# The last product of a hybrid encoder block as seven block products of sums, with its weights in quarters of 512 columns

## The chip, the cores and the metric

The kernel runs on one core of a Trainium2 chip. The metric is the time of one execution on the device in microseconds (us); lower is better. Several executions of the kernel before were timed, and one execution of it was profiled; its trace is what is read below. Engines: TensorE (PE in the profile; its weight loads are PEld), VectorE (DVE), ScalarE (ACT), GpSimd (POOL), SyncE (SP), which here only issues transfers.

## The reference

One layer: RMSNorm, one wide projection, sparse attention, a state-space layer, then two projections merged by sigmoid gates, the product with `w_out`, the residual and a final RMSNorm. Sequence 512, model width 2048, float32. What the change touches is the end:

```python
gates = jax.nn.sigmoid(merge + b_merge).reshape(bsz, l, N_BRANCH, D_MODEL)
mixed = gates[:, :, 0] * y_a + gates[:, :, 1] * y_b      # 512 x 2048
return x + mixed @ w_out                                 # w_out: 2048 x 2048
...
return rms_norm(x, g_final)
```

## The kernel before

Everything is kept transposed, channels on the 128 partitions and the 512 tokens along the free dimension, in 16 rows `k` of 128 channels. Each float32 operand is split in two parts, a rounded high part and the low rest, and each product is three matmuls (high by high, high by low, low by high), each with a 128x128 stationary and a 128x512 moving operand. The high part is made by ScalarE (a copy that rounds, `high_through`, L703), the low part by VectorE (a subtraction in place of the raw weights, `low_through`, L992). Weights stream in units of 128x2048 through three slots (`w_raw`, `w_hi`, `w_lo`; `w_raw` and `w_lo` are the same memory). SyncE issues the load of a unit when TensorE is done with the unit three before (`load`, L308). All orders are written out by hand: each engine has its list of instructions, and semaphores hold them together.

Before the last product comes `merge1`: 16 tiles of 128 channels (j = 0 to 15), each 48 matmuls. After each tile ScalarE makes the sigmoid gate (L709), VectorE multiplies and adds (L1380, L1381) and so finishes one row of `mixed` in `ya`. Rows of `ya` are then split by ScalarE (L923) and VectorE (`low_of_merge`, L1374).

The last product (`out_bank`, L655 to L657) runs in two halves of 1024 output columns. In a half all eight PSUM banks are in use: four tiles of 128 tokens by two of 512 columns. TensorE goes through k = 0 to 15, and for each k through all eight banks: 3 x 8 x 16 = 384 matmuls a half, 768 in all. The stationary operand is `mixed`, the moving one the weights. The last k rows of a half are done bank by bank, so that banks come free one after the other. VectorE adds each bank to the residual `res` (L1392), ScalarE takes the sums of squares (L951, L957, L961), and at the end of the second half VectorE and ScalarE scale the tokens (L1419 to L1424, L965) and SyncE stores them. `res` is loaded from `x` (L360) into the memory of `yb` once the merge is done, and the final gain `g_last` behind it (L363). GpSimd does nothing in this part.

## Time and profile before

| | us |
|---|---|
| time, median of 3 runs | 1188.05 (1187.62 to 1188.37) |
| the profiled execution, its own time | 1186.81 |
| span of its trace (first to last instruction) | 1185.0 |
| TensorE busy | 1158.0 (98%) |
| VectorE busy | 752.5 (64%) |
| ScalarE busy | 403.4 (34%) |
| GpSimd busy | 11.8 (1%) |

The span is 1.8 us shorter than the execution's own time. A matmul's record is longer than its place in the stream (they are pipelined), so TensorE's pace is read from the starts of consecutive matmuls. The same holds for back-to-back instructions of VectorE and ScalarE: a merged row with x12 gives the time of all twelve together. "Idle before" names who ended an engine's wait.

### The profile page before, as it was taken

The numbers are of one execution on the slowest core, as the hardware profiler recorded it, in microseconds if no ns is written. First come the engines' busy times: TensorE is split into PE (matmuls) and PEld (weight loads), VectorE is DVE, ScalarE is ACT, GpSimd is POOL, SyncE is SP. The second block draws the span as 40 slices with busy tenths as digits, with TensorE's granted clock in tenths as the row PEclk, the third lists the DMA queues.
The fourth block names the chain that finished last, engine by engine and source line by source line (L and its number), as shares of the span: only waits on it lengthen the run. The fifth ranks groups of instructions, "written<-read, shape, count | busy, mean of one in ns | idle before, by whom it ended". The sixth has DMA issues, their size and how long they took to land.

```text
span 1185.0 us, 13271 instructions
## 1 busy us (share of the span) xinstructions
PE 1158.0 (98%) x5357; PEld 949.8 (80%) x5357; DVE 752.5 (64%) x1317; ACT 403.4 (34%) x526; POOL 11.8 (1%) x12
## 2 busy tenths in 40 slices
PE   5999999999999999999999999999999999999997
PEld 4999888888777788887777777788888888887886
DVE  5887568999777778628999999443133343423324
ACT  7423243332376543332222323233222223313114
POOL 3000000000000000000000000000000000000000
PEclk9999999999999999999999999999999999999999
DMA  7444323223332237443433443332443343245223
GB/s 248 107 107 108 106 72 101 77 76 103 98 115 90 72 98 216 131 137 110 139 107 107 137 130 90 106 103 76 107 107 87 92 107 104 77 169 219 78 101 142
DMA packets 171885, 134.86 MB, mean 114 GB/s; under 512 B 10968, under 2 KB 158768, under 8 KB 170672
## 3 DMA queue, kind: packets, MB, share of 16 engines
q1 hardware_dynamic: 162912, 124.73, 36.1%
q10 hardware_dynamic: 8912, 9.29, 2.2%
q8 instruction: 42, 0.69, 0.2%
q14 instruction: 19, 0.16, 0.0%
HBM read 121.42 MB, written 12.58 MB: 113 GB/s over the span
## 4 chain that ended last, share of the span: by engine, by line
PE 83%; DVE 13%; DMA 1%; ACT 1%; issue 1%; SPq 0%; DVEq 0%; ACTq 0%
PE bank L405 21%; PE bank L407 20%; PE bank L406 20%; PE bank L655 5%; PE bank L657 5%; PE bank L656 5%; DVE w_lo L992 3%; DVE score L1097 2%; DVE small L1096 2%; PE bank L557 1%; PE bank L597 1%; PE bank L538 1%; DVE score L1085 1%; DMA xt<-in_x 1%; PE bank L547 1%
## 5 line engine op out<-in xcount | busy, mean ns | idle before, releaser
L405 PE MATMUL bank<-act_hi,w_hi 128*128 128x512 f32 (+1 forms) x1088 | 422.5, 388 | 2.6 <-DVE w_lo L992 2.6
L406 PE MATMUL bank<-act_lo,w_hi 128*128 128x512 f32 (+1 forms) x1088 | 416.9, 383 | 0.0
L407 PE MATMUL bank<-act_hi,w_lo 128*128 128x512 f32 (+1 forms) x1088 | 416.9, 383 | 0.0
L992 DVE TENSOR_TENSOR w_lo<-w_raw,w_hi 128x2048 fp32r<-128x2048 f32 x96 | 219.6, 2288 | 177.9 <-ACT w_hi L703 177.0
L703 ACT ACTIVATE w_hi<-w_raw 128x2048 fp32r<-128x2048 f32 (+1 forms) x97 | 184.8, 1905 | 184.1 <-DMA w_raw<-in_w_out 104.9
L405 PEld LDWEIGHTS bank<-act_hi,w_hi 128*128 128x128 f32 x1088 | 204.4, 188 | 48.5 <-issue 9.6
L407 PEld LDWEIGHTS bank<-act_hi,w_lo 128*128 128x128 f32 x1088 | 204.3, 188 | 38.5
L406 PEld LDWEIGHTS bank<-act_lo,w_hi 128*128 128x128 f32 x1088 | 204.5, 188 | 34.7
L655 PE MATMUL bank<-w_hi,act_hi 128*128 128x512 f32 x192 | 74.7, 389 | 0.0
L656 PE MATMUL bank<-w_lo,act_hi 128*128 128x512 f32 x192 | 74.7, 389 | 0.0
L657 PE MATMUL bank<-w_hi,act_lo 128*128 128x512 f32 x192 | 74.7, 389 | 0.0
L1380 DVE TENSOR_TENSOR gate<-gate,yb 128x512 f32<-128x512 f32 x16 | 11.1, 692 | 97.3 <-ACT gate L709 97.3
L709 ACT ACTIVATE gate<-bank,g_cols 128x512 f32<-128x512 f32 x16 | 11.0, 688 | 134.1 <-PE bank L407 134.1
L773 ACT ACTIVATE relu<-bank 128x256 f32<-128x256 f32 (+2 forms) x48 | 23.6, 492 | 90.9 <-PE bank L506 84.7
L405 PE MATMUL bank<-a_hi,w_hi 128*128 128x512 f32 x128 | 50.0, 390 | 0.0
L407 PE MATMUL bank<-a_hi,w_lo 128*128 128x512 f32 x128 | 49.8, 389 | 0.0
L406 PE MATMUL bank<-a_lo,w_hi 128*128 128x512 f32 x128 | 49.8, 389 | 0.0
L1085 DVE SCALAR_TENSOR_TENSOR score<-relu,w_idx,score 128x256 f32<-128x256 f32 (+2 forms) x45 | 27.8, 618 | 29.0 <-ACT relu L773 27.8
L656 PEld LDWEIGHTS bank<-w_lo,act_hi 128*128 128x128 f32 x192 | 36.0, 188 | 7.5
L655 PEld LDWEIGHTS bank<-w_hi,act_hi 128*128 128x128 f32 x192 | 36.0, 188 | 7.5
L657 PEld LDWEIGHTS bank<-w_hi,act_lo 128*128 128x128 f32 x192 | 36.0, 188 | 7.4
L405 PE MATMUL bank<-s_hi,w_hi 128*128 128x512 f32 x80 | 31.1, 389 | 0.0
(249 smaller groups left out, 1300.9 us busy)
## 6 DMA issues: line engine op xcount, KB each, us to landing
w_raw<-in_w_in SPq DMA_DIRECT2D x68, 1024.0 KB, 5.6
w_raw<-in_w_out SPq DMA_DIRECT2D x16, 1024.0 KB, 5.5
e_tables<-e_made ACTq DMA_DIRECT2D x16, 512.0 KB, 2.9
w_raw<-in_w_att_out SPq DMA_DIRECT2D x8, 1024.0 KB, 5.9
e_tab<-e_tables SPq DMA_DIRECT2D x16, 512.0 KB, 6.5
xt<-in_x SPq DMA_DIRECT2D x4, 1024.0 KB, 8.1
w_raw<-in_w_ssm_out SPq DMA_DIRECT2D x4, 1024.0 KB, 5.0
res<-in_x SPq DMA_DIRECT2D x4, 1024.0 KB, 11.7
```

The source lines that it names most:

```text
L405: nc.tensor.matmul(out_ap, wh, x_hi[k], start=(j == 0), stop=False)
L406: nc.tensor.matmul(out_ap, wh, x_lo[k], start=False, stop=False)
L407: last = nc.tensor.matmul(out_ap, wl, x_hi[k], start=False, stop=(j == n - 1))
L655: nc.tensor.matmul(out_ap, mh, w_hi[:, slot, w], start=(k == 0), stop=False)
L656: nc.tensor.matmul(out_ap, mh, w_lo[:, slot, w], start=False, stop=False)
L657: last = nc.tensor.matmul(out_ap, ml, w_hi[:, slot, w], start=False, stop=(k == KD - 1))
L703: nc.scalar.activation(w_hi[:, u % SLOTS, 0:n_el], w_raw[:, u % SLOTS, 0:n_el], ACT.Copy).then_inc(high_done, 1)
L773: nc.scalar.activation(relu[:, n % 2, 0:(b + 1) * P], pair_bank[n % 2][:, 0:(b + 1) * P], ACT.Relu, scale=IDX_DIM ** -0.5).then_inc(relu_d ...
L992: v.tensor_tensor(w_lo[:, u % SLOTS, :], w_raw[:, u % SLOTS, :], w_hi[:, u % SLOTS, :].bitcast(F32), ALU.subtract).then_inc(split_done, 1)
L1085: ins = v.scalar_tensor_tensor(scores[b], r, w, scores[b], ALU.mult, ALU.add)
L1096: link(v.max(small[:, 12:20], scores[b]))
L1097: link(v.match_replace(scores[b], small[:, 12:20], scores[b], REPLACED))
```

## The change

Rows (tokens) and columns of `mixed` and of the weights are cut in two, and per half of 1024 output columns the 2x2 block product is done with seven block products in place of eight, in Winograd's form of Strassen's scheme (15 sums). The two blocks in k are k = 0 to 7 and 8 to 15; those in tokens 0 to 255 and 256 to 511; those in columns two times 512.

- Four sums of `mixed` are made for each k of 0 to 7 (`sums_of`), in the memory of `yb`; the merge takes its rows in the order `MERGE_ORDER`, so that k and k + 8 are done together. Each operand is split as before.
- Weights are loaded in quarters of 128x512, in a ring of 12 (the same three slots). A half is 16 blocks of work: n = 0 to 7 with three quarters each (B11, B12, B22, from which two sums are made), n = 8 to 15 with four each (three sums); `turned` makes the sums on VectorE in place, then ScalarE and VectorE split each quarter. The second half is n = 16 to 31.
- The first eight blocks of a half fill six banks (products 1 to 3), the second eight use two more for product 4 and then reuse the six. Before that, `kept1`, `u2` and `u4` are taken out of them (ScalarE once, VectorE `mix`), and GpSimd adds them to `res`.
- The rows of `mixed` that are not split by the end of the merge are split between blocks 2 to 5 (`SPLIT_AT`).
- `res` is loaded in two halves, behind the quarters of block 7 (when all splits are done) and behind those of block 10. `g_last` is loaded behind the quarters of block 29.
- The last two blocks are done for 128-token tiles 0 and 2 first, then for 1 and 3; the tokens are finished in the order 2, 0, 3, 1.

The diff, cut to its core, indented less by twelve blanks:

```diff
-("ssmout", 4, 4), ("merge1", 14, 1), ("out", 16, 1)]
+("ssmout", 4, 4), ("merge1", 14, 1), ("out", 0, 1)]
 EARLY = 2
+HALF_K = KD // 2
+MERGE_ORDER = [0, 1, HALF_K, HALF_K + 1] + [k + HALF_K * i for k in range(2, HALF_K) for i in range(2)]
+RING = 4 * SLOTS
+HALVES = SEQ // 2
...
+def block_at(n):
+    half, second, k = n // (2 * HALF_K), n // HALF_K % 2, n % HALF_K
...
-        LAST_UNIT = UNIT0["out"] + 16
+        LAST_UNIT = UNIT0["out"]
+        BLOCKS = 4 * HALF_K
+        LAST_ORDER = (3, 0, 1, 2)
+        SPLIT_ORDER = [(0, k) for k in range(5)] + [(0, 5), (1, 0), (1, 1), (0, 6), (1, 2), (1, 3), (0, 7), (1, 4), (1, 5), (1, 6), (1, 7)]
+        SPLIT_AT = {2: SPLIT_ORDER[5:8], 3: SPLIT_ORDER[8:11], 4: SPLIT_ORDER[11:14], 5: SPLIT_ORDER[14:16]}
+        LAST_TOKENS = (2, 0, 3, 1)
+        a_banks, b_banks, c_banks, d_banks = banks[0:2], banks[2:4], banks[4:6], banks[6:8]
...
+def load_quarter(g, k, col):
+    if g < RING:
+        sp.wait_ge(tile_done, tiles_through(LAST_UNIT - SLOTS + g // 4))
+    else:
+        sp.wait_ge(q_done, 2 * (g - RING + 1))
+    slot, part = ring(g)
+    sp.dma_start(w_raw[:, slot, part], w_out_v[:, k, col:col + 512]).then_inc(q_loaded[g % RING], 16)
...
+for n in range(BLOCKS):
+    half, second, k = block_at(n)
+    b11, b12, b21, b22 = ((k + HALF_K * i, half * HALF + 512 * j) for i in range(2) for j in range(2))
+    for i, (kk, col) in enumerate((b11, b21, b22, b12) if second else (b11, b12, b22)):
+        load_quarter(quarter_at(n) + i, kk, col)
+    if n == 7:
+        sp.wait_ge(m_low, 2 * HALF_K)
+        load_res(0, range(TOK))
+    if n == 10:
+        load_res(1, range(TOK))
+    if n == BLOCKS - 3:
+        sp.wait_ge(shared_added, 16)
+        sp.dma_start(g_last[:, :], g_final.rearrange("(a d) -> a d", a=1).to_broadcast([P, D])).then_inc(gf_loaded, 16)
...
+for half in range(2):
+    pool.wait_ge(res_loaded[half], 16 * TOK)
+    if half:
+        pool.wait_ge(bank_taken, 8)
+    col = half * HALF
+    for ready, sources, into in ((p1_saved, kept1, ((0, 0),)), (u2_made, u2, ((2, 0),)), (u4_made, u4, ((0, 512), (2, 512)))):
+        for tb in range(2):
+            pool.wait_ge(ready, 2 * half + tb + 1)
+            for t, c in into:
+                part = res[:, t + tb, col + c:col + c + 512]
+                pool.tensor_tensor(part, part, sources[:, tb, :], ALU.add).then_inc(shared_added, 1)
...
+def first_pass(n, i, tb):
+    half, _, k = block_at(n)
...
+    if half == 1 and k == 0:
+        pe.wait_ge(bank_taken, (4, 6, 8)[i])
+    return block_product(bank[tb], quarter_at(n) + i, m_hi, m_lo, k == 0, k == HALF_K - 1)
+def second_pass(n, i, tb):
+    half, _, k = block_at(n)
...
+    if k == 0:
+        if i == 0 and half == 1:
+            pe.wait_ge(bank_taken, 2)
+        if i >= 1:
+            pe.wait_ge((p1_saved, u4_made, u2_made)[i - 1], 2 * half + 2)
+    return block_product(bank[tb], quarter_at(n) + i, m_hi, m_lo, k == 0, k == HALF_K - 1)
+for n in range(BLOCKS - 2):
+    half, second, k = block_at(n)
+    if n == 0:
+        pe.wait_ge(tile_free, TILE0["out"])
     if half == 0:
+        pe.wait_ge(m_low, SPLIT_ORDER.index((second, k)) + 1)
+    for i in range(4 if second else 3):
+        pe.wait_ge(q_split, quarter_at(n) + i + 1)
+        for tb in range(2):
+            (second_pass if second else first_pass)(n, i, tb).then_inc(q_done, 1)
+for tb in range(2):
+    for n in (BLOCKS - 2, BLOCKS - 1):
+        pe.wait_ge(q_split, quarter_at(n) + 4)
+        for i in LAST_ORDER:
+            second_pass(n, i, tb).then_inc(q_done, 1)
...
+def high_of_first(k):
+    act.wait_ge(sums_made, 2 * k + 2)
+    nc.scalar.activation(ya_r[:, k, HALVES:SEQ], ya[:, k, 0:HALVES], ACT.Copy)
+    nc.scalar.activation(sums12(k)[0], yb[:, k, :], ACT.Copy).then_inc(m_high, 1)
+def high_of_second(k):
+    row = HALF_K + k
+    nc.scalar.activation(act_hi[:, row, :], ya[:, row, :], ACT.Copy)
+    nc.scalar.activation(act_lo[:, k, :], yb[:, row, :], ACT.Copy).then_inc(m_high, 1)
+def high_of_quarters(n):
+    second = block_at(n)[1]
+    for i in range(4 if second else 3):
+        g = quarter_at(n) + i
+        slot, part = ring(g)
+        made = ((3, 0, 0, 1) if second else (0, 1, 2))[i]
+        if made:
+            act.wait_ge(t_made, turned_at(n) + made)
+        else:
+            act.wait_ge(q_loaded[g % RING], 16 * (g // RING + 1))
+        nc.scalar.activation(w_hi[:, slot, part], w_raw[:, slot, part], ACT.Copy).then_inc(q_high, 1)
...
+for n in range(2, BLOCKS):
+    half, second, k = block_at(n)
+    high_of_quarters(n)
+    for which, kk in SPLIT_AT.get(n, ()):
+        (high_of_first, high_of_second)[which](kk)
+    if second and k == 1:
+        if half:
+            act.wait_ge(shared_added, 8)
+        for tb in range(2):
+            act.wait_ge(q_done, done_at(n - 2, 0, tb))
+            nc.scalar.activation(kept1[:, tb, :], a_banks[tb][:, :], ACT.Copy).then_inc(p1_saved, 1)
...
+def sums_of(k):
...
+    v.tensor_tensor(s3, a11, a21, ALU.subtract)
+    link(v.tensor_tensor(s1, a21, a22, ALU.add))
+    v.tensor_tensor(s2, s1, a11, ALU.subtract).then_inc(sums_made, 1)
+    dve.wait_ge(sums_made, 2 * k + 1)
+    v.tensor_tensor(s4, a12, s2, ALU.subtract).then_inc(sums_made, 1)
+def low_of_first(k):
+    hi, lo = sums12(k)
+    dve.wait_ge(m_high, SPLIT_ORDER.index((0, k)) + 1)
+    v.tensor_tensor(ya_r[:, k, 0:HALVES], ya[:, k, 0:HALVES], ya_r[:, k, HALVES:SEQ].bitcast(F32), ALU.subtract)
+    v.tensor_tensor(lo, yb[:, k, :], hi.bitcast(F32), ALU.subtract).then_inc(m_low, 1)
+def low_of_second(k):
+    row = HALF_K + k
+    dve.wait_ge(sums_made, 2 * k + 2)
+    dve.wait_ge(m_high, SPLIT_ORDER.index((1, k)) + 1)
+    v.tensor_tensor(ya_r[:, row, :], ya[:, row, :], act_hi[:, row, :].bitcast(F32), ALU.subtract)
+    v.tensor_tensor(act_lo[:, row, :], yb[:, row, :], act_lo[:, k, :].bitcast(F32), ALU.subtract).then_inc(m_low, 1)
+def turned(n):
+    second = block_at(n)[1]
+    g, t0 = quarter_at(n), turned_at(n)
+    w = [w_raw[:, ring(g + i)[0], ring(g + i)[1]] for i in range(4 if second else 3)]
+    def loaded(i):
+        dve.wait_ge(q_loaded[(g + i) % RING], 16 * ((g + i) // RING + 1))
+    if second:
+        b11, b21, b22, b12 = w
+        loaded(2)
+        loaded(3)
+        v.tensor_tensor(b12, b22, b12, ALU.subtract).then_inc(t_made, 1)
+        loaded(0)
+        dve.wait_ge(t_made, t0 + 1)
+        v.tensor_tensor(b11, b11, b12, ALU.add).then_inc(t_made, 1)
+        loaded(1)
+        dve.wait_ge(t_made, t0 + 2)
+        v.tensor_tensor(b11, b21, b11, ALU.subtract).then_inc(t_made, 1)
+    else:
+        b11, b12, b22 = w
+        loaded(0)
+        loaded(1)
+        v.tensor_tensor(b12, b12, b11, ALU.subtract).then_inc(t_made, 1)
+        loaded(2)
+        dve.wait_ge(t_made, t0 + 1)
+        v.tensor_tensor(b22, b22, b12, ALU.subtract).then_inc(t_made, 1)
+def low_of_quarters(n):
+    for i in range(4 if block_at(n)[1] else 3):
+        g = quarter_at(n) + i
+        slot, part = ring(g)
+        dve.wait_ge(q_high, g + 1)
+        v.tensor_tensor(w_lo[:, slot, part], w_raw[:, slot, part], w_hi[:, slot, part].bitcast(F32), ALU.subtract
+                        ).then_inc(q_split, 1)
...
+    if j == KD - 1:
+        for n in range(2):
+            turned(n)
+            low_of_quarters(n)
...
+    if j == EARLY or j % 2 == 1 and j > EARLY:
+        dve.wait_ge(gate_used, KD + j + 1)
+        sums_of(j // 2 - (j == EARLY))
...
+low_of_first(4)
+turned(2)
...
+def mix(half):
+    n = 2 * HALF_K * half + HALF_K - 1
+    if half:
+        dve.wait_ge(shared_added, 8)
+    for tb in range(2):
+        dve.wait_ge(q_done, done_at(n, 2, tb))
+        dve.wait_ge(p1_saved, 2 * half + tb + 1)
+        v.tensor_tensor(u2[:, tb, :], b_banks[tb][:, :], kept1[:, tb, :], ALU.add).then_inc(u2_made, 1)
+    for tb in range(2):
+        dve.wait_ge(u2_made, 2 * half + tb + 1)
+        v.tensor_tensor(u4[:, tb, :], c_banks[tb][:, :], u2[:, tb, :], ALU.add).then_inc(u4_made, 1)
...
+for n in range(2, BLOCKS):
+    half, second, k = block_at(n)
+    low_of_quarters(n)
+    for which, kk in SPLIT_AT.get(n, ()):
+        (low_of_first, low_of_second)[which](kk)
+    if second and k == 1:
+        mix(half)
+    if n == 2 * HALF_K + 1:
+        take_first_half()
+    if n >= BLOCKS - 2:
+        dve.wait_ge(gf_loaded, 16)
+        dve.wait_ge(first_squared, 2 * TOK)
+        for t in (2 * (n - BLOCKS + 2), 2 * (n - BLOCKS + 2) + 1):
+            v.tensor_tensor(res[:, t, 0:HALF], res[:, t, 0:HALF], g_last[:, 0:HALF], ALU.mult).then_inc(first_scaled, 1)
+    if n + 1 < BLOCKS:
+        turned(n + 1)
...
+def late_tokens(tb):
+    t, i = 2 + tb, 2 * tb
+    if tb:
+        dve.wait_ge(final_rest_done, i - 1)
+    bank = last_bank(tb, 3)
+    add_part(t, HALF + 512, bank).then_inc(part_ready, 1)
+    link(add_part(t, HALF, bank))
+    dve.wait_ge(part_ready, 2 * i + 1)
+    multiplied(i, t, HALF + 512)
+    add_part(t, HALF, last_bank(tb, 0)).then_inc(part_ready, 1)
+    dve.wait_ge(part_ready, 2 * i + 2)
+    multiplied(i, t, HALF)
+def early_tokens(tb):
+    t, i = tb, 2 * tb + 1
+    if tb:
+        dve.wait_ge(final_rest_done, i - 1)
+    for c, b in ((0, 1), (1, 2)):
+        add_part(t, HALF + 512 * c, last_bank(tb, b)).then_inc(part_ready, 1)
+        dve.wait_ge(part_ready, 2 * i + c + 1)
+        multiplied(i, t, HALF + 512 * c)
...
+dve.wait_ge(shared_added, 16)
+late_tokens(0)
+early_tokens(0)
+finish(0)
+late_tokens(1)
+finish(1)
+early_tokens(1)
+finish(2)
+finish(3)
```

How the instructions stand. On VectorE behind the last gate (L1380 and L1381 before, L1570 and L1571 after). Before (L992 splits a unit of weights, L1374 a row of `mixed`, L1392 takes a bank):

```order
L1380 TENSOR_TENSOR gate<-gate,yb 128x512 [waits tile_free]
L1381 TENSOR_TENSOR ya<-ya,gate 128x512 [waits v_step]
L992 TENSOR_TENSOR w_lo<-w_raw,w_hi 128x2048 [waits high_done]
L1374 TENSOR_TENSOR act_lo<-ya,act_hi 128x512 [waits m_high] x12
L992 TENSOR_TENSOR w_lo<-w_raw,w_hi 128x2048 [waits high_done] x6
L1396 MEMSET small 128x1 x4
```

After, the blocks 3 and 4 in the same place (L1545 and L1548 make sums of weights, L1556 splits quarters, L1510 to L1519 split `mixed` and its sums):

```order
L1545 TENSOR_TENSOR w_raw<-w_raw 128x512 [waits q_loaded10,q_loaded9]
L1548 TENSOR_TENSOR w_raw<-w_raw 128x512 [waits t_made,q_loaded11]
L1556 TENSOR_TENSOR w_lo<-w_raw,w_hi 128x512 [waits q_high] x3
L1510 TENSOR_TENSOR ya_r<-ya,ya_r 128x256 [waits m_high]
L1511 TENSOR_TENSOR act_hi<-yb,act_hi 128x512
L1518 TENSOR_TENSOR ya_r<-ya,act_hi 128x512 [waits m_high,sums_made]
L1519 TENSOR_TENSOR act_lo<-yb,act_lo 128x512
L1518 TENSOR_TENSOR ya_r<-ya,act_hi 128x512 [waits m_high,sums_made]
L1519 TENSOR_TENSOR act_lo<-yb,act_lo 128x512
L1545 TENSOR_TENSOR w_raw<-w_raw 128x512 [waits q_loaded1,q_loaded0]
L1548 TENSOR_TENSOR w_raw<-w_raw 128x512 [waits t_made,q_loaded2]
L1556 TENSOR_TENSOR w_lo<-w_raw,w_hi 128x512 [waits q_high] x3
```

The twelve splits of `mixed` in one run became splits of two and two rows between the weights of consecutive blocks, and each block's weights have sums ahead of their splits.

On TensorE at a point where banks change hands. Before, the start of the second half (`bank_taken` counts VectorE's additions):

```order
L655 MATMUL bank2<-w_hi_53,s_hi_112 128x512 [waits bank_taken,split_done]
L655 MATMUL bank3<-w_hi_53,s_hi_112 128x512 [waits bank_taken]
L655 MATMUL bank4<-w_hi_53,s_hi_112 128x512 [waits bank_taken]
L655 MATMUL bank5<-w_hi_53,s_hi_112 128x512 [waits bank_taken]
L655 MATMUL bank6<-w_hi_53,s_hi_112 128x512 [waits bank_taken]
```

After, the first matmuls of block 8 on six of its eight banks (block 24 reads alike), each the first of three:

```order
L724 MATMUL bank6<-w_hi_53,act_hi_49 128x512 [waits q_split,m_low]
...
L724 MATMUL bank0<-w_hi_53,act_hi_49 128x512 [waits p1_saved,q_split]
...
L724 MATMUL bank1<-w_hi_53,act_hi_49 128x512 [waits p1_saved]
...
L724 MATMUL bank4<-w_hi_53,act_lo_50 128x512 [waits u4_made,q_split]
...
L724 MATMUL bank5<-w_hi_53,act_lo_50 128x512 [waits u4_made]
...
L724 MATMUL bank2<-w_hi_53,act_lo_50 128x512 [waits u2_made,q_split]
```

TensorE now waits in the middle of a half too, for a copy of ScalarE (`p1_saved`) and four additions of VectorE (`u2_made`, `u4_made`).

On SyncE, whose transfers go out in this order. Before, from the weights of the last product on:

```order
L308 DMA w_raw<-in_w_out 128x2x1024 [waits tile_done] x8
L360 DMA res<-in_x 128x2048 [waits gate_used]
L360 DMA res<-in_x 128x2048 x3
L363 DMA g_last<-in_g_final 128x2048 [waits m_low]
L308 DMA w_raw<-in_w_out 128x2x1024 [waits tile_done] x8
```

After:

```order
L410 DMA w_raw<-in_w_out 128x512 [waits tile_done] x12
L410 DMA w_raw<-in_w_out 128x512 [waits q_done] x12
L414 DMA res<-in_x 128x1024 [waits m_low]
L414 DMA res<-in_x 128x1024 x3
L410 DMA w_raw<-in_w_out 128x512 [waits q_done] x12
L414 DMA res<-in_x 128x1024 x4
L410 DMA w_raw<-in_w_out 128x512 [waits q_done] x68
L429 DMA g_last<-in_g_final 128x2048 [waits shared_added]
L410 DMA w_raw<-in_w_out 128x512 [waits q_done] x8
```

16 loads of weights became 112 of a quarter of the size (28 units' worth in place of 16), and the residual's first half stands ahead of the weights of block 8.

## Rows read from the trace of the kernel before

**Rows 1.** The page: its first line and busy time of two engines (us, share, instructions)

```profile
span 1185.0 us, 13271 instructions
PE 1158.0 (98%) x5357; PEld 949.8 (80%) x5357; DVE 752.5 (64%) x1317; ACT 403.4 (34%) x526; POOL 11.8 (1%) x12
```

**Rows 2.** The page: the chain that ended last, by engine

```profile
PE 83%; DVE 13%; DMA 1%; ACT 1%; issue 1%; SPq 0%; DVEq 0%; ACTq 0%
```

**Rows 3.** Windows: stretch, length, busy PE, PEld, DVE, ACT, POOL, clock, DMA share, GB/s

```profile
1000.00:1050.00 50.00, 50.00 (x223) 41.40 (x222) 19.98 (x19) 16.30 (x18) 0.00 (x0) 1.00 0.33 100
...
1100.00:1150.00 50.00, 50.00 (x222) 41.43 (x221) 11.57 (x6) 7.67 (x4) 0.00 (x0) 1.00 0.35 105
```

**Rows 4.** Timeline, PE, ACT and DVE at the last merge tile (start, length, what, idle)

```profile
1002.13 0.39 PE L407 MATMUL bank<-act_hi,w_lo 128*128 128x512 f32 x1
...
1002.36 0.39 PE L655 MATMUL bank<-w_hi,s_hi 128*128 128x512 f32 x1
...
1002.62 0.69 ACT L709 ACTIVATE gate<-bank,g_cols 128x512 f32<-128x512 f32 x1 [8.38 <-PE bank L407]
...
1003.34 0.69 DVE L1380 TENSOR_TENSOR gate<-gate,yb 128x512 f32<-128x512 f32 x1 [6.78 <-ACT gate L709]
...
1004.06 0.69 DVE L1381 TENSOR_TENSOR ya<-ya,gate 128x512 f32<-128x512 f32 x1
```

**Rows 5.** Timeline of the tail: TensorE's last matmul, VectorE and ScalarE behind it

```profile
1177.27 0.39 PE L657 MATMUL bank<-w_hi,act_lo 128*128 128x512 f32 x1
1177.76 0.69 DVE L1392 TENSOR_TENSOR res<-bank,res 128x512 f32<-128x512 f32 x1 [1.22 <-PE bank L657]
...
1179.90 1.15 ACT L965 ACTIVATE res<-fin,small 128x1024 f32<-128x1024 f32 x1 [0.30 <-DVE small L1421]
```

**Rows 6.** Timelines of DVE and ACT: twelve instructions back to back

```profile
1007.35 7.30 DVE L1374 TENSOR_TENSOR act_lo<-ya,act_hi 128x512 fp32r<-128x512 f32 x12
...
1005.01 6.35 ACT L923 ACTIVATE act_hi<-ya 128x512 fp32r<-128x512 f32 x12
```

**Rows 7.** Groups by form from 960 us on (busy us, mean ns, idle before)

```profile
L992 DVE TENSOR_TENSOR w_lo<-w_raw,w_hi 128x2048 fp32r<-128x2048 f32 x19 | 43.5, 2290 | 97.6 <-ACT w_hi L703 97.6
...
L1392 DVE TENSOR_TENSOR res<-bank,res 128x512 f32<-128x512 f32 x16 | 10.4, 683 | 7.4 <-PE bank L657 7.3
...
L1409 DVE TENSOR_TENSOR res<-res,g_last 128x1024 f32<-128x1024 f32 x4 | 4.6, 1219 | 2.4 <-ACT square_out L951 2.4
```

**Rows 8.** Groups by form, VectorE, the whole span: 256 columns

```profile
L1141 DVE TENSOR_TENSOR e_temp<-e_base,rot 128x256 f32<-128x256 f32 x4 | 1.7, 424 | 0.1
```

**Rows 9.** Timeline, PE between the two halves

```profile
1089.17 0.39 PE L657 MATMUL bank<-w_hi,act_lo 128*128 128x512 f32 x1
1090.35 0.47 PE L655 MATMUL bank<-w_hi,s_hi 128*128 128x512 f32 x1 [0.80 <-DVE res L1392]
```

**Rows 10.** The page: issues, KB each and us from issue to landing

```profile
w_raw<-in_w_out SPq DMA_DIRECT2D x16, 1024.0 KB, 5.5
```

**Rows 11.** Timelines of SP and ACT around the loads of the residual

```profile
1057.36 2.42 SPq L360 DMA_DIRECT2D res<-in_x  x4
...
1067.83 0.38 SPq L308 DMA_DIRECT2D w_raw<-in_w_out  x1
...
1078.89 1.92 ACT L703 ACTIVATE w_hi<-w_raw 128x2048 fp32r<-128x2048 f32 x1 [14.12 <-DMA w_raw<-in_w_out]
```

**Rows 12.** Windows while the residual is loaded (columns as in Rows 3)

```profile
1064.00:1066.00 2.00, 2.00 (x10) 1.68 (x9) 1.20 (x1) 0.77 (x1) 0.00 (x0) 1.00 0.97 410
```

**Rows 13.** Windows behind TensorE's last matmul (columns as in Rows 3)

```profile
1179.00:1180.00 1.00, 0.00 (x0) 0.00 (x0) 0.45 (x3) 0.67 (x4) 0.00 (x0) 0.93 0.00 0
1180.00:1181.00 1.00, 0.00 (x0) 0.00 (x0) 0.65 (x1) 1.00 (x1) 0.00 (x0) 0.50 0.00 0
```

**Rows 14.** Timeline, POOL: its longest instruction

```profile
23.55 4.60 POOL L395 TENSOR_TENSOR w_lo<-w_raw,w_hi 128x2048 fp32r<-128x2048 f32 x1
```

240 lines of the change are left out of this document (116 added, 124 removed).

## The prediction

> **What bounds the kernel now.** I read the page first. TensorE is busy for 98% of the span [rows 1], and the chain that ended last runs over it for 83% and over VectorE for 13% [rows 2]. Then the windows of the stage that changes: from 1000 us on TensorE has no gap, VectorE works 20 of 50 us, later 11.6, and ScalarE 16 and 8 [rows 3]. So the stage is TensorE's, and fewer matmuls would shorten it, as long as the others keep up. The timelines give its length. The last product starts at 1002.36, one slot behind the last merge matmul [rows 4]; the last matmul of its first half starts at 1089.17 [rows 9]: 384 matmuls in 87.04 us, 0.2267 us each. The second half starts at 1090.35, after a gap of 0.95 us behind VectorE's additions, and its last matmul at 1177.27 ends its slot at 1177.50 [rows 5, 9]. From there to the end of the span are 7.5 us. The stage takes 182.64 us from 1002.36 to 1185.0; I count from 1002.36 as zero.
>
> **What it saves.** Seven products for eight: 32 blocks, half with three and half with four products, six matmuls each, are 672 matmuls for 768. 96 x 0.2267 = 21.8 us. A block of the first kind (n = 0 to 7, 16 to 23) takes TensorE 18 x 0.2267 = 4.08 us, of the second kind 5.44.
>
> **What VectorE must do for a block.** Its additions of 128x512 take 0.69 alone, 0.60 back to back (twelve in 7.30 [rows 6]) and 0.72 start to start where the second waits for the first (1003.34 to 1004.06 [rows 4]). First kind: one sum that the next waits for, one more, three low parts: 0.72 + 0.60 + 3 x 0.60 = 3.12. Second kind: three sums in a chain end after 2 x 0.72 + 0.69 = 2.13; only then ScalarE may round the quarter that it has first in its order (0.62 by the twelve in 6.35 [rows 6], 0.03 for each hand-over [rows 4]), so the first low part starts at 2.81, and four make 5.21. Before, a unit cost 2.29 per 10.9 us of TensorE [rows 7]. VectorE is now at 3.12 of 4.08 and 5.21 of 5.44: anything more comes out of its lead. Added up with no wait at all, VectorE's list is: 2.4 (the last gate), 1.6 (the last four sums), 0.9 (a split), 14 x 3.12 = 43.7, 16 x 5.21 = 83.4, splits 12.4 (below), two mixes 4.8, ten additions from banks 6.0, four multiplications 4.6 (1.14 back to back, 1.22 alone [rows 7]), then 22.6 for the last tokens (below): 182.4, which is the 182.6 of before. So the change can hardly gain even if VectorE never waits.
>
> **Start, +1.1.** Product 1 goes into the banks that the merge's gates are read from, so TensorE waits for the last gate, which ends at 1003.31 [rows 4], and starts at 1.07. Before it began with other banks. Blocks 0 and 1 are turned and split ahead of the last gate, where VectorE has 6.8 us idle [rows 4].
>
> **Blocks 3 to 6, +6.4.** Behind the last gate VectorE has the four sums (256 columns, 0.42 each [rows 8], 1.6 with their waits) and a split (0.34 + 0.60), and begins block 2 at 4.9. A split of the first kind is 0.94, of the second 1.20; blocks 2, 3 and 4 carry 3.34 of these each, block 5 2.40. So VectorE begins block 3 at 11.4, 4 at 17.9, 5 at 24.3, 6 at 29.8, 7 at 33.0, 8 at 36.1; the first quarter is ready 2.0 later and TensorE starts 0.1 behind that. TensorE wants blocks 3, 4, 5, 6 at 13.3, 17.6, 24.1 and 30.5 and gets them at 13.5, 20.0, 26.5 and 32.0: waits of 0.2, 2.4, 2.4 and 1.4. It ends block 7 at 40.1. Before, the twelve splits ran in one piece under matmuls that had their weights.
>
> **Block 8, the load, +3.7.** SyncE waits for the last split (29.9), issues four loads of `res` (0.6 each [rows 11]), then the quarters of block 8. What a queue does behind such loads is in the trace: weights issued at 1067.83 behind them arrived at 1078.9, 11 us, while alone a unit lands in 5.5 [rows 10, 11]; bytes moved at 410 GB/s [rows 12]. 2.1 MB and 1.05 MB at that rate are 7.7 us, from about 31.9 (1.9 after the issue; 5.5 less 2.6 for the bytes leaves 2.9, of which I put 1.9 ahead and 0.7 behind) to 40.2. Without the load VectorE would start at 36.1. The first quarter is ready at 43.7, TensorE waits 3.7. If the queue let the weights pass, this would be 0.
>
> **Block 8, the banks, +6.6.** Products 2 and on in block 8 wait for ScalarE's `kept1`, which stands behind all of block 9 in its list, and for four additions of VectorE, also behind block 9. VectorE starts block 9 at 45.4, ScalarE ends its last quarter at 49.8 and the two copies at 51.0; TensorE had stopped at 45.2: 5.9. VectorE ends the additions at 53.1: 0.7 more. Then it is ahead, and 7 blocks run at 5.44.
>
> **Clock, +1.0.** After the last matmul the granted clock was 0.93 in the slice from 1179 and 0.50 after [rows 13]: it fell from 2.4 to 1.2 GHz some 2.2 us after the last matmul ended. So it falls in the 5.9 too, and the six matmuls behind take about twice as long, partly under the 0.7. I take 1.0, bounds 0 and 3. The waits of 2.4 may do it as well, but VectorE is the later one there.
>
> **Half to half, -0.25.** VectorE takes ten additions between the halves, and most can go while TensorE still works on the later products; I find 0.7 of waiting, for the last two banks, against 0.95 before.
>
> **Block 24, +2.7.** The same two waits as in block 8, with VectorE ahead this time: the ring frees block 25's last quarters when block 22 is half done, their loads take 3, so VectorE starts 25 some 2.4 before block 24 begins, and TensorE waits 2.0 for the copies and 0.7 for the additions.
>
> **Last blocks, +2.4.** Block 31 of the first token tile wants all its quarters 2.7 behind the start of block 30. VectorE has two multiplications by the gain (2.3) ahead of it and gets them ready at 5.1.
>
> **The last tokens, +9.0.** VectorE is free of block 31 and its multiplications 7.2 after the start of block 30. Then it does 18 linked instructions for the four tokens, and twice waits for ScalarE to free `fin`: the third token starts at 15.1, the fourth at 20.3, the last scaling on ScalarE (1.15 [rows 5]) ends at 25.8, and from there to the end it was 3.95 before (1181.05 to 1185.0): 29.8, with TensorE's end at 13.3. That is 16.5 behind the last matmul, 7.5 before.
>
> **Sum.** -21.8 + 1.1 + 6.4 + 3.7 + 6.6 + 1.0 - 0.25 + 2.7 + 2.4 + 9.0 = +10.9. The profiled execution took 1186.81, 1.2 below the median; so 1197.7 for it, and 1199 for the median. Everything before 1002 is as it was: the extra sums and splits in the merge (1.6 + 0.94 for every two tiles) fit in VectorE's idle time (6.78 a tile [rows 4]).
>
> **Rivals.**
> *GpSimd slows VectorE.* GpSimd adds 16 times 128x512 to `res`; by its 4.60 for 2048 columns [rows 14] that is 1.15 each. No row here shows it beside a two-input instruction of VectorE from memory, so its cost to VectorE is between 0 and all of it. Six of eight in a half fall on such instructions: 6.9 us. VectorE's lead behind block 9 is about 4.9, so some 2 are lost in each half, and as VectorE then has no slack left, block 30 comes 3.6 late: +7.6, that is 1206.5. The Trainium skill (SBUF — State Buffer, "two separate sides") says the two share a port pair under an exclusive lock when VectorE reads two inputs from this memory and GpSimd reads it too, and whoever comes second waits for the whole instruction. By that rule this rival is what happens; against it, GpSimd may be the one that waits.
> *The waits are milder.* The load of `res` doesn't hold up block 8, the clock doesn't fall, ScalarE's copies overlap better: what is left is VectorE's list, +0 to +6, some 1192.
> *TensorE stays the bound.* If VectorE's small instructions overlap more than 0.60 each, so that a block with splits costs it under 4.08 and block 31 is ready on time, all stalls go but the start and the tail: -21.8 + 1.1 + 9.0 = -11.7, 1176.3, faster. It decides at 4.08 us per block with splits (6.46 by the rows), which the rows speak against.
> *It doesn't do what it says.* TensorE's list is 96 rows shorter, so this is out.
>
> **How the numbers follow.** The forecast (1195 to 1203) 0.45; GpSimd 0.27; milder 0.17; TensorE-bound 0.05; something dearer than all this (over 1210) 0.06. The range 1190 to 1209 leaves the last two and the ends of others out. A difference under 0.2% (2.4 us) can't be told from none. Faster 0.05; same, from the low end of the milder case, 0.05; slower 0.90.
>
> **What would show it.** In the profile after: 96 matmuls fewer at the same 0.227; TensorE idle behind `w_lo` in blocks 4 to 6 by 1 to 3 us each, behind a load in block 8, then some 6 behind `kept`; VectorE at 90% and more in the stage; a clock below 1 near the wait for `kept`; a tail of about 16 us. GpSimd's additions longer than 1.2 us, or VectorE's of 0.69 stretched to 1.8, would be the first rival. Wrong it would be if TensorE had no gaps in the first half.

## The result, and the profile after

| | before | after |
|---|---|---|
| time, median (lowest to highest) of 4 | 1187.84 us (1187.46 to 1188.37) | 1214.11 us (1213.93 to 1215.02) |
| ratio, 95% interval | | 1.0222 (1.0205 to 1.0240), slower |
| span of the trace | 1185.0 us | 1212.4 us |

The change costs 26.3 us. The forecast was 11 us, with a range up to 1209; the direction was right, the size was not.

The page of the changed kernel: span, busy time, and the chain that ended last.

```profile
span 1212.4 us, 13655 instructions
...
PE 1148.7 (95%) x5261; PEld 937.4 (77%) x5261; DVE 875.6 (72%) x1553; ACT 444.5 (37%) x642; POOL 37.7 (3%) x28
...
PE 70%; DVE 23%; ACT 3%; issue 2%; DMA 2%; SPq 0%; ACTq 0%; DVEq 0%
```

TensorE has 96 matmuls fewer, 5261 for 5357 [rows 1]. But VectorE's part of the chain is 23% instead of 13% [rows 2]: the engine that worked in TensorE's shadow now sets part of the time. The windows over the changed stage (columns as in Rows 3) show it:

```profile
1000.00:1050.00 50.00, 37.71 (x161) 29.37 (x159) 39.39 (x68) 24.82 (x47) 0.00 (x0) 0.99 0.58 186
1050.00:1100.00 50.00, 45.71 (x183) 36.93 (x184) 43.55 (x61) 19.27 (x36) 12.96 (x8) 0.87 0.61 195
1100.00:1150.00 50.00, 43.95 (x179) 35.02 (x178) 43.26 (x67) 17.35 (x30) 6.50 (x5) 0.93 0.51 157
```

Where [rows 3] had TensorE busy for all of 50 us with 222 or 223 matmuls, there are 160 to 183 now, VectorE works 39 to 44 us of 50 instead of 12 to 20, and the granted clock is 0.87 in the middle. Where TensorE stood is read from its timeline. All its waits of 1.3 us and more in the stage are these; in brackets the idle time and who ended it. The last row is its last matmul.

```profile
1023.71 0.47 PE L724 MATMUL bank<-w_hi,ya_r 128*128 128x512 f32 x1 [2.19 <-DVE w_lo L1556]
1030.27 0.47 PE L724 MATMUL bank<-w_hi,ya_r 128*128 128x512 f32 x1 [2.18 <-DVE w_lo L1556]
1035.97 0.47 PE L724 MATMUL bank<-w_hi,ya_r 128*128 128x512 f32 x1 [1.36 <-DVE w_lo L1556]
1049.93 0.77 PE L724 MATMUL bank<-w_hi,act_hi 128*128 128x512 f32 x1 [5.56 <-DVE w_lo L1556]
1050.50 0.63 PE L725 MATMUL bank<-w_lo,act_hi 128*128 128x512 f32 x1
1050.92 0.63 PE L726 MATMUL bank<-w_hi,ya_r 128*128 128x512 f32 x1
...
1057.12 0.76 PE L724 MATMUL bank<-w_hi,act_hi 128*128 128x512 f32 x1 [4.29 <-DVE w_lo L1556]
...
1106.04 0.47 PE L724 MATMUL bank<-w_hi,ya_r 128*128 128x512 f32 x1 [3.77 <-DVE res L1584]
...
1143.96 0.47 PE L724 MATMUL bank<-w_hi,act_hi 128*128 128x512 f32 x1 [2.06 <-DVE w_lo L1556]
...
1186.29 0.79 PE L724 MATMUL bank<-w_hi,act_lo 128*128 128x512 f32 x1 [4.62 <-DVE w_lo L1556]
...
1195.71 0.39 PE L726 MATMUL bank<-w_hi,act_lo 128*128 128x512 f32 x1
```

Every wait names VectorE. (At 1057.12 the name stands for the ScalarE copies: the matmul waited for `p1_saved`, and `kept1` ended at 1056.97.) Behind five of the longer waits the matmuls start some 0.43 us apart (1050.50 to 1050.92), not 0.227. Now the ledger (what each term of the sum took), counted from the end of the last merge matmul's slot as in the prediction; that end is 1003.42, where it was 1002.36. This 1.06 us is a difference between executions and not a cost of the change: in the traces of the versions below, which are the same up to there, the end lies anywhere from 1002.30 to 1004.15. A gap is counted above the pace of 0.2267:

| term | forecast | measured |
|---|---|---|
| 96 matmuls fewer | -21.8 | -21.8 |
| start | +1.1 | +1.0 |
| blocks 3 to 6 | +6.4 | +6.5 |
| block 8, load | +3.7 | +5.7 |
| block 8, banks | +6.6 | +4.7 |
| half to half | -0.25 | +3.0 |
| block 24 | +2.7 | +2.8 |
| blocks 30 and 31 | +2.4 | +6.2 |
| matmuls at half rate | +1.0 | +9.3 |
| tail | +9.0 | +9.0 |
| sum | +10.9 | +26.4 |

The stage takes 208.98 us instead of 182.64. Five terms came out within 0.1. Those that failed are the load, the banks, the boundary between the halves, the last blocks, and the clock. TensorE's list says where it stood, though, not why. The term that grew most, the matmuls at half rate, is tested below in block 8, and there it cost nothing.

The second reading is VectorE's own. Its timeline and GpSimd's behind block 9:

```profile
1053.09 0.69 DVE L1540 TENSOR_TENSOR w_raw<-w_raw 128x512 f32<-128x512 f32 x1
1054.48 2.50 DVE L1556 TENSOR_TENSOR w_lo<-w_raw,w_hi 128x512 fp32r<-128x512 f32 x4 [0.69 <-ACT w_hi L1028]
...
1060.07 1.59 DVE L1537 TENSOR_TENSOR w_raw<-w_raw 128x512 f32<-128x512 f32 x1
1061.76 1.58 DVE L1540 TENSOR_TENSOR w_raw<-w_raw 128x512 f32<-128x512 f32 x1
1064.04 6.10 DVE L1556 TENSOR_TENSOR w_lo<-w_raw,w_hi 128x512 fp32r<-128x512 f32 x4 [0.70 <-ACT w_hi L1028]
1070.06 0.68 DVE L1534 TENSOR_TENSOR w_raw<-w_raw 128x512 f32<-128x512 f32 x1
```

```profile
1059.31 10.29 POOL L473 TENSOR_TENSOR res<-res,u 128x512 f32<-128x512 f32 x6
```

While GpSimd adds shared parts to `res` (1.7 us each), a sum takes VectorE 1.59 instead of 0.69 and four low parts 6.10 instead of 2.50. Its turn from sum to sum is 10.8 us (1059.29 to 1070.06) and 5.39 elsewhere: 5.4 us lost, and as much again from 1146 on. TensorE ran from 1057 to 1102 without a wait all the same, as the first low part of block 10 was ready 4.4 us before TensorE took it; that of block 11 was only 1.2 us ahead, and that of block 15 1.4. In all of the stage VectorE never waits for a matmul directly. It waits for loads: 10.0 us, of which 5.88 at block 8:

```profile
1046.11 0.69 DVE L1534 TENSOR_TENSOR w_raw<-w_raw 128x512 f32<-128x512 f32 x1 [5.88 <-DMA w_raw<-in_w_out]
```

How long a load takes from issue to landing tells its two kinds of waits apart. Of the quarters of `w_out`, first all in the page, then the four of block 8, issued right behind the residual:

```profile
w_raw<-in_w_out SPq DMA_DIRECT2D x112, 256.0 KB, 3.3
...
w_raw<-in_w_out SPq DMA_DIRECT2D x4, 256.0 KB, 8.1
```

The weights of block 8 were queued behind the residual's bytes. Those of block 24, for which VectorE waits 2.93, were not: they landed 3.1 after their issue, but were issued late, as TensorE had to free the slots of the ring first. In this way TensorE does hold VectorE back, by some 3.5 us in all.

So VectorE's list can be added up too: the 182.4 forecast, plus 10.0 for loads, 10.8 of stretching, and 4.0 of pace (a block of the second kind takes 5.39 where 5.21 was forecast, 16 times, and one of the first 3.20 for 3.12, 14 times): 207.2 of 208.98. Of the remaining 1.8, 1.5 lie behind the last scaling: it ends at 1206.99 and the span at 1212.4, 5.4 later, where it was 3.95 before. ScalarE's last two scalings, and SyncE's last store:

```profile
1204.82 2.17 ACT L1052 ACTIVATE res<-fin,small 128x1024 f32<-128x1024 f32 x2
...
1207.20 1.18 SPq L434 DMA_DIRECT2D out_dram<-res  x1
```

### The profile page after: what moved, and what is told of

Same layout as the page of the kernel before. It is cut to its first block, busy times and chain, and to the rows that moved or that the text cites. A ratio compares the mean times of both kernels' runs of the same rounds, so it can differ in the third digit from the quotient of the medians.

```text
span 1212.4 us, 13655 instructions
## 1 busy us (share of the span) xinstructions
PE 1148.7 (95%) x5261; PEld 937.4 (77%) x5261; DVE 875.6 (72%) x1553; ACT 444.5 (37%) x642; POOL 37.7 (3%) x28
## 4 chain that ended last, share of the span: by engine, by line
PE 70%; DVE 23%; ACT 3%; issue 2%; DMA 2%; SPq 0%; ACTq 0%; DVEq 0%
PE bank L483 20%; PE bank L484 20%; PE bank L485 20%; DVE w_lo L1556 4%; DVE w_lo L1117 3%; DVE score L1222 2%; DVE small L1221 2%; PE bank L635 1%; PE bank L675 1%; PE bank L616 1%; DVE w_raw L1540 1%; DVE w_raw L1537 1%; DVE score L1210 1%; DMA w_raw<-in_w_out 1%; DMA xt<-in_x 1%
## 5 line engine op out<-in xcount | busy, mean ns | idle before, releaser
L1117 DVE TENSOR_TENSOR w_lo<-w_raw,w_hi 128x2048 fp32r<-128x2048 f32 x80 | 182.9, 2287 | 77.6 <-ACT w_hi L789 76.8
L789 ACT ACTIVATE w_hi<-w_raw 128x2048 fp32r<-128x2048 f32 (+1 forms) x81 | 154.2, 1903 | 77.9 <-DMA w_raw<-in_w_in 75.5
L1028 ACT ACTIVATE w_hi<-w_raw 128x512 fp32r<-128x512 f32 x112 | 64.3, 623 | 104.8 <-DVE w_raw L1540 71.0
L1556 DVE TENSOR_TENSOR w_lo<-w_raw,w_hi 128x512 fp32r<-128x512 f32 x112 | 77.4, 749 | 11.2 <-ACT w_hi L1028 11.2
L1570 DVE TENSOR_TENSOR gate<-gate,yb 128x512 f32<-128x512 f32 x16 | 11.1, 692 | 83.6 <-ACT gate L795 83.6
L724 PE MATMUL bank<-w_hi,act_hi 128*128 128x512 f32 x96 | 39.2, 408 | 11.9 <-DVE w_lo L1556 11.9
L473 POOL TENSOR_TENSOR res<-res,kept 128x512 f32<-128x512 f32 x4 | 5.4, 1380 | 1102.4 <-ACT kept L1068 1102.4
L726 PE MATMUL bank<-w_hi,ya_r 128*128 128x512 f32 x96 | 39.1, 407 | 0.0
L725 PE MATMUL bank<-w_lo,act_hi 128*128 128x512 f32 x96 | 38.8, 404 | 0.0
L724 PE MATMUL bank<-w_hi,act_lo 128*128 128x512 f32 x64 | 26.7, 418 | 6.1 <-DVE w_lo L1556 5.8
```

What stands on the lines that cost most here:

```text
L724: nc.tensor.matmul(bank[:, :], m_hi, w_hi[:, slot, part], start=start, stop=False)
L725: nc.tensor.matmul(bank[:, :], m_hi, w_lo[:, slot, part], start=False, stop=False)
L726: return nc.tensor.matmul(bank[:, :], m_lo, w_hi[:, slot, part], start=False, stop=stop)
L789: nc.scalar.activation(w_hi[:, u % SLOTS, 0:n_el], w_raw[:, u % SLOTS, 0:n_el], ACT.Copy).then_inc(high_done, 1)
L1028: nc.scalar.activation(w_hi[:, slot, part], w_raw[:, slot, part], ACT.Copy).then_inc(q_high, 1)
L1117: v.tensor_tensor(w_lo[:, u % SLOTS, :], w_raw[:, u % SLOTS, :], w_hi[:, u % SLOTS, :].bitcast(F32), ALU.subtract).then_inc(split_done, 1)
```

## The experiments

Theory: VectorE's list is the bound of the whole stage, so what comes off it comes off the time, except where it then waits for loads. Rival: TensorE's own stops (banks, loads, clock) add up. Times are medians; the changed kernel is at 1214.1, the kernel before at 1187.4 to 1187.9 beside every run. Ratios with their intervals are to the kernel before. "Stage" is the time from the end of the last merge matmul's slot to the end of the span in the trace, 208.98 for the changed kernel. It leaves out the differences between executions ahead of it, but is of one execution.

**GpSimd's additions cut.**

```diff
-part = res[:, t + tb, col + c:col + c + 512]
+part = res[:, t + tb, col + c:col + c + 1]
-pool.tensor_tensor(part, part, sources[:, tb, :], ALU.add)
+pool.tensor_tensor(part, part, sources[:, tb, 0:1], ALU.add)
```

> GpSimd's sixteen additions to the residual are cut from 512 columns to one each; the rest of the shared parts is left out of the output, and nothing else changes. Theory (VectorE sets the pace of this stage, and GpSimd's eight additions per half, 1.37 to 1.7 us each, stretch VectorE's instructions beside them; block 9 and block 25 took 10.8 us instead of 5.39, so VectorE loses 5.4 us of its lead in each half): the wait of 3.9 us between the halves and that of 4.8 us in block 31 shrink to under 1 us, the half-rate matmuls behind them go too, and the time is 8 to 10 us below the changed kernel's 1214.1, so 1204 to 1206. Rival (TensorE's waits for loads and copies set the end, and VectorE only follows them): 0 to 2 us below, over 1212.

GpSimd's additions here leave most of the shared parts out of the result. 1208.8 us (ratio 1.0179, 1.0164 to 1.0194): 5.3 less, between the two. The groups by form of VectorE from 1003 us on (busy, mean ns, idle before), first of the changed kernel, then of this one:

```profile
L1556 DVE TENSOR_TENSOR w_lo<-w_raw,w_hi 128x512 fp32r<-128x512 f32 x106 | 73.6, 753 | 11.2 <-ACT w_hi L1028 11.2
L1537 DVE TENSOR_TENSOR w_raw<-w_raw 128x512 f32<-128x512 f32 x16 | 12.9, 804 | 1.7
...
L1534 DVE TENSOR_TENSOR w_raw<-w_raw 128x512 f32<-128x512 f32 x16 | 10.9, 684 | 8.8 <-DMA w_raw<-in_w_out 8.8
```

```profile
L1556 DVE TENSOR_TENSOR w_lo<-w_raw,w_hi 128x512 fp32r<-128x512 f32 x106 | 66.4, 687 | 11.2 <-ACT w_hi L1028 11.2
...
L1537 DVE TENSOR_TENSOR w_raw<-w_raw 128x512 f32<-128x512 f32 x16 | 11.1, 693 | 1.7
...
L1534 DVE TENSOR_TENSOR w_raw<-w_raw 128x512 f32<-128x512 f32 x16 | 11.0, 688 | 14.5 <-DMA w_raw<-in_w_out 14.5
```

Low parts fall by 7.2 us, the two sums (L1540 reads like L1537) by 1.8 each: 10.8 of stretching are gone. Waits for loads rise from 10.0 to 15.0 (here 14.5, and 0.5 at L1548). 10.8 less 5.0 is 5.8, the span fell by 5.3. One of the new waits is block 11's:

```profile
1067.53 0.69 DVE L1534 TENSOR_TENSOR w_raw<-w_raw 128x512 f32<-128x512 f32 x1 [3.04 <-DMA w_raw<-in_w_out]
```

The last quarter it waited for was issued at 1064.1 and landed in the usual time, when the residual had long landed (1057.8):

```profile
w_raw<-in_w_out SPq DMA_DIRECT2D x1, 256.0 KB, 3.3
```

So this wait is for a slot of the ring, which TensorE, held up in block 8, freed late. A VectorE that gets ahead meets the ring. A larger ring was not tried.

**The residual loaded later.**

```diff
-if n == 7:
+if n == 10:
     sp.wait_ge(m_low, 2 * HALF_K)
     load_res(0, range(TOK))
-if n == 10:
+if n == 12:
     load_res(1, range(TOK))
```

> The two loads of the residual go out behind the weights of blocks 10 and 12 instead of 7 and 10. Theory (the wait of 5.7 us at the start of block 8 is for weights queued behind 2.1 MB of residual; VectorE stood 5.9 us for them): the wait falls to 1 us or less and the matmuls at half rate behind it go; as VectorE is then earlier by up to 5.9 us in everything that follows, the time falls by 5 to 7 us, to 1207 to 1209. Rival (the load only moves the stall: blocks 11 to 13 wait for their weights, or GpSimd gets the residual later and its additions fall beside other blocks): 0 to 2 us, over 1212.

1210.7 us (1.0195, 1.0178 to 1.0212): 3.4 less, under what I expected. The wait of 5.7 at the start of block 8 is gone; that for the banks behind it is 5.4 instead of 4.3. In VectorE's groups its waits for loads fall from 10.0 to 4.7, and it loses 2.1 to more stretching (all first, second and third sums of the second-kind blocks: 12.1, 12.9 and 13.8 us instead of 10.9, 12.9 and 12.9), as GpSimd, served its residual later, now runs into another block. 5.3 less 2.1 is 3.2.

**Copies and mixes earlier.** In ScalarE's and VectorE's lists:

```diff
-if second and k == 1:
+if second and k == 0:
     mix(half)
```

> ScalarE's two copies of product 1 and VectorE's four additions stand behind block 8 (and 24) in their lists, in place of block 9 (and 25). Theory (TensorE's waits of 4.7 us in block 8 and 2.8 us in block 24 exist only because these six instructions stand behind a whole further block): both waits fall to about 1 us, with the half-rate matmuls behind them. But VectorE is the engine with least slack, and its list is as long as before, so only what it gains by not waiting later counts: I expect 3 to 6 us below 1214.1, so 1208 to 1211. Rival (the end is set by VectorE's list and GpSimd's additions, and this only moves TensorE's waits to the half boundary and block 31): under 1 us.

1214.3 us (1.0226, 1.0211 to 1.0241): nothing; the rival was right. The wait of 4.7 in block 8 is gone, and others have come, as VectorE's list is no shorter:

```profile
1058.11 0.47 PE L724 MATMUL bank<-w_hi,act_hi 128*128 128x512 f32 x1 [1.59 <-DVE w_lo L1556]
...
1066.78 0.47 PE L724 MATMUL bank<-w_hi,act_hi 128*128 128x512 f32 x1 [2.01 <-DVE w_lo L1556]
```

**The clock held up.** 40 matmuls without use are put into the two waits of block 8; one bank's result is then not the product.

```diff
 for i in range(4 if second else 3):
+    if n == HALF_K and i < 2:
+        for d in range((22, 18)[i]):
+            nc.tensor.matmul(banks[7][:, :], act_hi[:, HALF_K, 0:P], act_hi[:, HALF_K, :], ...)
     pe.wait_ge(q_split, quarter_at(n) + i + 1)
```

> 40 matmuls without use are put on TensorE in block 8, 22 ahead of its first product and 18 ahead of its second, some 5.0 and 4.1 us at full rate, inside the two waits of 5.7 and 4.7 us there; the second group goes into an open sum of products, so one bank of the output is not the product. Nothing else is changed. Both theories expect the granted clock to stay near 1 between 1040 and 1070 instead of 0.50 in 1050 to 1060, and the 20 matmuls behind the waits to start 0.227 instead of 0.427 apart. Theory that the half-rate stretches cost time (20 x 0.2 us = 4 us in block 8): 2 to 4 us less. Rival (VectorE sets the end, TensorE's lost rate in block 8 is regained in the wait between the halves): within 1 us of 1214.1, and that wait grows from 3.9 by the microseconds gained.

1214.5 us (1.0224, 1.0209 to 1.0239): nothing. TensorE from the first added group on:

```profile
1043.30 5.15 PE L762 MATMUL bank<-act_hi 128*128 128x512 f32 x22
1048.38 0.50 PE L724 MATMUL bank<-w_hi,act_hi 128*128 128x512 f32 x1
1048.71 0.40 PE L725 MATMUL bank<-w_lo,act_hi 128*128 128x512 f32 x1
1048.95 0.40 PE L726 MATMUL bank<-w_hi,ya_r 128*128 128x512 f32 x1
...
1104.62 0.47 PE L724 MATMUL bank<-w_hi,ya_r 128*128 128x512 f32 x1 [4.72 <-DVE res L1588]
```

The matmuls behind the wait start 0.24 apart, the granted clock is 1.00 from 1040 to 1070 (in the changed kernel 0.96, 0.50 and 0.86 in these three windows of 10 us). What TensorE gained it waited for later: 4.72 between the halves for 3.77, and new waits of 0.79 and 0.50. The half rate in block 8 was a symptom. The run tests no more than block 8, some 4 of the 9.3 us: in its trace other matmuls ran at half rate instead, 8 behind the wait at 1022.78 and 14 behind that of block 31 (7 in the changed kernel), and at the last tokens VectorE waited 0.91 for a matmul, which it does not do in the changed kernel.

**Late loads and early mixes together.** 

> The late loads of the residual and the early copies and mixes together, with the sums of weights where the changed kernel has them. The first alone gave 3.4 us, the second nothing. Theory (VectorE has no slack: what is taken from its waits counts, what is taken from TensorE's does not): no more than the first alone, 1209 to 1212. Rival (the two waits in block 8 cover for each other: with one gone the other stays, with both gone TensorE runs through, and the whole 10.4 us of gaps there comes off): 1202 to 1206.

1209.0 us (1.0179, 1.0162 to 1.0196), 1.7 below the late loads alone, at the theory's lower end.

**The third sum cut.** VectorE's list alone made shorter:

```diff
-v.tensor_tensor(b11, b21, b11, ALU.subtract).then_inc(t_made, 1)
+v.tensor_tensor(b11[:, 0:1], b21[:, 0:1], b11[:, 0:1], ALU.subtract).then_inc(t_made, 1)
```

> The third of VectorE's sums for a block of the second kind is cut from 512 columns to one (its product's result is then not the product); all waits and the order stay. It takes some 0.5 to 0.6 us off VectorE's list in each of sixteen blocks, 8 to 9 us in all. In the trace of the changed kernel VectorE never waits for TensorE in the stage; it waits for weights at block 8 (5.9 us) and near block 24 (3.9 together), and nowhere else. Theory (VectorE's list sets the end, so what is taken off it comes off the time, save where VectorE then waits for loads): blocks 9 to 15 and 25 to 31, 7 to 8 us, less 0 to 2: 1206 to 1209. Rival (as the woven sums showed, something else holds the stage: loads behind the ring of quarters): 0 to 2 us, over 1212.

1205.4 us (1.0148, 1.0133 to 1.0164): 8.7 less, 0.6 below the expected range. This instruction now counts

```profile
L1540 DVE TENSOR_TENSOR w_raw<-w_raw 128x1 f32<-128x1 f32 x16 | 4.4, 273 | 1.7
```

instead of 12.9 us: 8.5 off the list, 8.7 off the time. In the trace the stage is 201.58, 7.4 less, with 0.8 more of waiting for loads; so some 1.3 of the 8.7 is the spread between executions, and 8.5 less 0.8 still agrees with 7.4. This is the cleanest of the tests: nothing of TensorE, loads or order was touched, and its rival (at most 2 us) is out.

**Everything light.** Late loads, early mixes and GpSimd's cut: 

> Late loads of the residual, early copies and mixes, and GpSimd's additions cut to one column (the rest of the shared parts left out). The first two alone gave 1209.0, GpSimd's cut alone 5.3 us of the 10.8 by which VectorE's instructions were stretched, since VectorE then waited 5.3 us longer for loads. Theory (VectorE's list, with the waits for loads that are left): with the residual out of the way in block 8 more of the 10.8 comes off: 6 to 10 us below 1209.0, 1199 to 1203. Rival (VectorE waits for loads in every place where it gets ahead): 3 us or less, over 1206.

1199.95 us (1.0104, 1.0088 to 1.0119): 9.1 below the version with GpSimd's full additions.

With the third sum cut as well: 

> Late loads, early mixes, GpSimd cut to one column, and the third sum cut to one column: the last two leave parts of the result out. Without the last cut it took 1199.95; that cut alone gave 8.7 us. Theory (VectorE still bounds the stage there: TensorE waited 4.9 us between the halves and 1.4 and 4.8 in blocks 30 and 31): 5 to 8.7 us less, 1191.3 to 1195. Rival (at 4.86 us a block VectorE gets ahead of TensorE's 5.44 and waits for loads instead): 3 us less or fewer, over 1197.

1194.0 us (1.0051, 1.0034 to 1.0068): 6.0 less. VectorE waits for TensorE once (2.04 at the mix of block 24; 1.48 there in the version before), so its list is no longer the only bound.

With the gain's multiplications cut and three `fin` buffers: 

> As the last, with the gain's four multiplications cut to one column too and three buffers for the last tokens. Theory: some 26 us of VectorE's 208 are gone then, and the stage nears its parts that no list of VectorE makes shorter: 152.3 of matmuls, 1.0 at the start, 5 in blocks 3 to 6, 1 to 3 in each mix, 15 in the tail; a stage of 175 to 180, 1180 to 1187 in all, the first below the kernel before. Rival (loads and banks hold it): within 3 us of the last, over 1189.

1190.2 us (1.0023, 1.0012 to 1.0034; 1188.1 to 1193.0 in seven executions): 3.8 less, a miss of 3 us and more against the 1180 to 1187 expected. About 5.4 us less of work brought 3.8. The profiled execution is the slowest of the seven; in it VectorE's wait for block 13's weights, behind the second load of the residual, was 3.07 for 1.55, and between the halves TensorE still waits 3.75 us, for additions that stand behind block 17 in VectorE's list. So even without some 25 us of what VectorE did (10.8 of stretching, 8.5, 4.0 and 1.4), the seven products stay slower than the eight, if by 0.2% only.

**The gain's multiplications cut alone.** 

> VectorE's four multiplications by the gain behind blocks 30 and 31 are cut from 1024 columns to one (the first halves of the rows stay without the gain). It takes some 4 us off VectorE's list, two of them ahead of block 31 and two ahead of the last tokens. Theory (VectorE's list sets the end, and the 4.8 us for which TensorE waits in block 31 are mostly these two and no lead left to cover them): the wait falls to about 2.6, the tail starts 2 us earlier for VectorE as well: 3.5 to 4.5 us below 1214.1, 1209.6 to 1210.6. Rival (the last tokens wait for TensorE's banks, not for VectorE): 1 to 2.2 us below.

1211.0 us (1.0194, 1.0179 to 1.0209): 3.1 less. Block 31's first matmul, and VectorE at the last tokens:

```profile
1184.11 0.50 PE L724 MATMUL bank<-w_hi,act_lo 128*128 128x512 f32 x1 [2.52 <-DVE w_lo L1556]
```

```profile
1185.33 1.29 DVE L1584 TENSOR_TENSOR res<-bank,res 128x512 f32<-128x512 f32 x2 [1.14 <-PE bank L726]
```

The wait falls from 4.62 to 2.52, as expected. The time is 0.4 us short of the expected 3.5 to 4.5. VectorE waits 1.14 for a bank, so part of the second pair of multiplications had been hidden; hence 3.1, not 4. With that work gone the last tokens wait for TensorE, as the rival had it, and the result lies between the two.

**Sums woven into low parts.** On paper this makes VectorE's list shorter: low, sum, low, sum, so no chain of sums and no wait for ScalarE.

```diff
-low_of_quarters(n)
+low_of_quarters(n, turned(n + 1) if n + 1 < BLOCKS else iter(()))  # one sum behind each low part
```

> VectorE's sums of the next block's weights stand between the low parts of this block (low, sum, low, sum, ...) instead of behind them; the work and all else are as in the changed kernel. In that kernel a block of the second kind costs VectorE 5.39 us, of which 0.70 is a wait for ScalarE's first rounding and some 0.5 the hand-overs of three sums in a chain; woven, seven instructions at 0.60 are 4.2. Theory (VectorE's list is what bounds the stage; TensorE needs 5.44 per such block, so VectorE regains 1.2 us of lead in each): the wait between the halves falls from 3.9 to 1 us or less, those of blocks 30 and 31 (1.4 and 4.8) to under 1 together, and the half-rate matmuls behind them go; the waits of blocks 3 to 6 and block 8 stay. 8 to 11 us below 1214.1: 1203 to 1206. Rival (quarters are loaded only as TensorE frees the ring, so VectorE cannot get ahead and waits for loads instead): 0 to 3 us below, over 1211.

1224.4 us (1.0305, 1.0290 to 1.0321): 10.3 slower, neither theory. Seven instructions do take 4.2 us in a row, and this is what they then wait for:

```profile
L1559 DVE TENSOR_TENSOR w_lo<-w_raw,w_hi 128x512 fp32r<-128x512 f32 x106 | 75.3, 720 | 2.5 <-ACT w_hi L1028 1.4
...
L1534 DVE TENSOR_TENSOR w_raw<-w_raw 128x512 f32<-128x512 f32 x16 | 11.1, 691 | 38.2 <-DMA w_raw<-in_w_out 38.2
```

```profile
1045.49 0.69 DVE L1534 TENSOR_TENSOR w_raw<-w_raw 128x512 f32<-128x512 f32 x1 [8.56 <-DMA w_raw<-in_w_out]
...
1063.19 1.41 DVE L1559 TENSOR_TENSOR w_lo<-w_raw,w_hi 128x512 fp32r<-128x512 f32 x1
1071.34 0.69 DVE L1534 TENSOR_TENSOR w_raw<-w_raw 128x512 f32<-128x512 f32 x1 [6.74 <-DMA w_raw<-in_w_out]
```

42.6 us of waiting for loads (38.2, and 4.4 at L1547) instead of 10.0. A sum of block n + 1 now stands ahead of low parts of block n; if its weights are late, the finished roundings of block n wait behind it, TensorE with them, and TensorE is what frees the ring's slots. The traces bear this out: the last quarter of block 11 was issued at 1068.36 and landed 2.9 later, so the 6.74 were spent waiting for its slot, not for bytes; the 8.56 at block 8 were for bytes (8.1 from issue to landing). What the order saved, some 22 us (5 of them less stretching), was more than lost to a dependence that it had added.

Woven with late loads and early mixes: 

> Woven sums, late loads of the residual, and early copies and mixes together. Theory (VectorE's list bounds the changed kernel; with 1.2 us less of it per block of the second kind the stage becomes TensorE's, and then the order of copies and mixes counts too): what is left beside 672 matmuls at 0.2267 (152.3) is 1.0 at the start, some 6 in blocks 3 to 6, 2 to 5 in blocks 8 and 24, 1 to 2 between the halves, and the tail of 16.5: a stage of 179 to 183 instead of 209, 1184 to 1190 in all, about the kernel before's 1187.4. Rival (the gains only add up: that of the woven sums and the 3.4 of the late loads, nothing for the mixes): 1198 to 1202.

1207.9 us (1.0167, 1.0152 to 1.0183), 1.1 below the same without weaving, 18 above the expected range and 6 above the rival's: a plain miss. With three `fin` buffers: 

> As the last, and the last tokens have three buffers instead of two for the products with the gain, so VectorE does not wait twice for ScalarE to free one (0.91 and 0.50 us in the changed kernel's trace). Expected of both theories: 1 to 1.5 us less than without it, if VectorE's chain sets the tail.

1206.3 us (1.0155, 1.0139 to 1.0170), 1.6 less, near what was expected. This is the fastest version that does all the work.

With the residual in eight single loads behind blocks 8 to 15: 

> The residual is loaded one token tile of 512 KB at a time, behind the weights of blocks 8 to 15; besides woven sums, early copies and mixes, and three buffers at the end. With the loads in two bursts this version took 1206.3, with VectorE waiting 3.5 us for the weights of block 11 behind a burst and TensorE 1.9 twice there. Theory (a burst of residual is what makes the woven order stall): that wait goes, 2 to 5 us less: 1201 to 1204. Rival (GpSimd's additions stretch VectorE there anyway, and the waits only move): within 1.5 us of 1206.3.

1209.8 us (1.0187, 1.0170 to 1.0203), 3.6 slower, which neither side expected: VectorE still waits 3.60 for block 11's weights (3.8 from issue to landing, so it is the slot again), and the burst was not the cause of that wait. In the traces the stage grew by 4.0 us: VectorE's busy time by 2.7 (GpSimd's additions now stretch 15.8 us instead of 13.1) and its waits for loads by 1.7.

And with GpSimd cut: 

> As the last, with GpSimd's additions cut to one column each (shared parts left out). It shows what the seven products could reach if their shared parts cost VectorE nothing. Theory (VectorE's list plus contention): 3 to 8 us less than the last, 1194 to 1200, still above the 1187.9 of the kernel before, as the tail (16.5 against 7.5 behind the last matmul), blocks 3 to 6 (4 to 6) and the mixes (2 to 4 each) stay. Rival (contention is now hidden in VectorE's regained lead): within 1.5 us of the last.

1198.1 us (1.0088, 1.0073 to 1.0103): 11.7 less, more than the theory's 8. GpSimd's additions stretched VectorE more in this version (15.8 us) than in the changed kernel (10.8), and 6.8 us of new waits for loads take part of it back. The traces show 8.6 less; this version's four executions spread over 4.2 us, and the profiled one is the slowest.

No version that computes everything beats the kernel before.

## Why the forecast was wrong

**What held.** The saving, the start, blocks 3 to 6 (0.3, 2.3, 2.35 and 1.5 for 0.2, 2.4, 2.4 and 1.4) and block 24, each from rows of before. So did the remark that VectorE's list alone, 182.4, was as long as the stage of before. The tail is 16.5 behind the last matmul as forecast, but by luck: the last tokens took VectorE and the stores 24.0 instead of 22.6 (the 1.5 behind the last scaling), and began 7.5 before TensorE's end instead of 6.1.

**The step that failed: "Then it is ahead, and 7 blocks run at 5.44."** The forecast summed TensorE's stops, took VectorE as ahead after block 9, and put the small waits of the half boundary and of blocks 30 and 31 on that lead. The seven blocks did run without a wait. But the lead was used up in block 10 (4.4 us before, 1.2 behind) and in block 26 (3.6 and 0.3), and it was missing where the half ends. Two things took it, and the sum had neither:

- GpSimd's additions. This was the first rival, at 0.27, priced at +7.6 for bounds of 0 and 6.9 us in a half. The traces show 5.4 in a half, 10.8 in all; taking it away gave 5.3 us in the changed kernel, 9.1 with late loads and early mixes, and 11.7 in the spread and woven version. The prediction named the Trainium skill (SBUF — State Buffer, "two separate sides"), by which an instruction of VectorE with two inputs from this memory and one of GpSimd exclude each other for a whole instruction. The rows fit it: 0.69 became 1.59, and GpSimd's took 1.7. The forecast priced this rival at the lead lost and no more, since it still counted on slack behind it.
- The pace. 5.39 us for a second-kind block, not 5.21, against TensorE's 5.44: a start-to-start of 0.79 where a sum waits for the one before (0.72 was read from a pair in [rows 4]). Small, 4.0 us in all, but it took the slack in which lead would have been regained. No version tests its share alone.

**The terms that follow from it.** Half to half, 3.0 above before instead of 0.25 below: VectorE began its ten additions 1.3 us after TensorE had run out (1103.42, the slot of the last matmul of block 15 ended at 1102.1), where the forecast's 0.7 of waiting needs it some 2 ahead. Blocks 30 and 31, 6.2 for 2.4: without lead the two multiplications (2.3), three sums, the wait for ScalarE and four low parts are 7.66 us from block to block, and TensorE covers 2.72 of them. The cut of the multiplications confirms their share. The load of block 8 was 5.7 for 3.7; delaying the residual removed it. Here only the size of the term was off: VectorE began at 1046.11, 42.7 behind zero, where I had 40.2. The bytes moved at 322 to 387 GB/s from 1038 to 1046, not at 410, which makes some 1.2 of it; and of the 2.9 that the sum put beside the bytes, its parts (1.9 and 0.7) leave 0.3 out. The banks took 4.7 for 6.6: TensorE stopped at 49.0 instead of 45.2, the copies ended at 53.55 instead of 51.0, and there was no second wait for the additions.

**The clock: right sign, wrong size, and in block 8 not a cause.** Waits of 2.1 and of 3.8 to 5.6 us were followed by 6 to 14 matmuls at 1.2 GHz, 9.3 us in TensorE's ledger for 1.0 forecast. But full rate in block 8 gave nothing back. Had I mis-sized only this, the forecast would have been near for a wrong reason: adding it to a sum of TensorE's stops is double counting where another engine sets the pace.

**What stays open.** The half-rate matmuls outside block 8, which no run took away by themselves; 0.3 us of VectorE's list; and what a larger ring would give, since part of each version's waits for loads is for slots that TensorE frees late.

## What to carry to other kernels

When a change moves work onto an engine until its list is as long as the stage, stop summing only the waits of the old bound: write the new engine's ledger too, with its waits for loads and the stretching by neighbours, and let the longer one be the forecast. A slack of 1% per block (5.39 of 5.44) covers nothing: here each loss stayed until the end. When such an engine waits for a load, look at the time from issue to landing: if it is as long as always, the load was issued late, and more bandwidth would not help. And a shorter list is not a faster one if the new order puts an instruction that waits for a load ahead of work that others wait for (the woven sums: 22 us less work, 10 us slower).

## What the runs showed of the hardware that I had not expected

- A 128x512 addition of GpSimd (1.7 us each, 1.37 beside VectorE's additions from banks) and one of VectorE with both inputs from the on-chip memory (0.69 alone) keep step when both run: 1.58 and 1.59 us each for VectorE in the changed kernel, up to 1.78 in the woven one. The additions that read a bank (L1594, L1597) kept their 0.60 start to start beside GpSimd.
- The granted clock was not the same behind like waits: behind one of 2.2 us at 1023 it stayed at 1.00 in the changed kernel (window 1020 to 1030) and was 0.83 in the same window of the late-load version.
- Dependent 128x512 additions on VectorE start 0.79 us apart in a chain of three (1046.11, 1046.91, 1047.71), independent ones 0.60: the chain costs a third more.
- A 128x1 addition that waits for the one before still takes time: 0.27 us on average with only the third sum cut, 0.16 in the version with everything cut.
